# Expert loop of a mixture-of-experts tail: output products by column half, gather split around the second input products

## The chip, the cores and the metric

The program runs on one NeuronCore of a Trainium2 chip, everything in 32-bit floats. The time is the device time of one execution in microseconds (us). The kernel before was run three times: 1990.79, 1992.39 and 1993.29 us. Its trace is of a fourth execution, which took 1992.95 us.

## The reference, cut to what matters

The program is a two-layer mixer block followed by a second block whose feed-forward part is a mixture of 32 experts. Only that part is touched by the change. Each of 256 tokens goes to two experts:

```python
def expert_block(args):
    idx, w, e = args
    xb = tok_pad[idx]                                     # gathered tokens, 1024 wide
    hb = jax.nn.silu(xb @ ex_gate[e]) * (xb @ ex_up[e])   # 1024 -> 512
    return (hb @ ex_down[e]) * w[:, None]                 # 512 -> 1024
...
out = jnp.zeros((n + 1, d), y.dtype).at[tok_buf].add(y.reshape(buf, d))
...
x = _layernorm(ALPHA * x + g2 * ffn, ln2_g[l], ln2_b[l])
```

`g2` is a gate of 1024 values, one for each output column.

## The kernel before, in words

Tokens are sorted into blocks of 64 places (`PLACES`), each with one expert. A first block is done alone; then a loop (`pair_tensor` on TensorE, `pair_scalar` on ScalarE, `pair_vector` on VectorE, `pair_sync` on SyncE) takes two blocks in each iteration. With these inputs it runs 14 iterations. Each engine has its own instruction stream, and semaphores order them. VectorE's loop first counts through the unused steps of 20 possible ones and runs the body in the last 14.

An iteration on TensorE, in program order:

- `in_products(0)`, `in_products(1)` (L3396, L3397): for block j, gate and up products from the gathered tokens `xg`. Each takes a 128x64 tile of the array, one for the lower and one for the upper 64 PSUM partitions, and the two run side by side.
- `gathered(0)` (L3326): half of the gather for the next iteration, as a product of the tokens with the 0/1 matrix `chosen_at`, over the full 128x128 array. VectorE writes `chosen_at` in `choose` (L3507, L3511), in the same iteration.
- `hidden_turned` (L3407) and the transposes of the weights of the places (L3443), full array.
- `out_products(0)`, `out_products(1)` (L3421): for block j, both 512-column halves of the output, again in two 128x64 tiles side by side; block 0 goes to PSUM bank `("down", 0)`, block 1 to `("down", 1)`. In both banks a column half lies on 64 partitions.
- `gathered(1)` (L3326): the second half of the gather.
- four products that put the rows back to their tokens (L3453), full array.

ScalarE does silu (L3481), and copies the transposes and the gather out of PSUM (L3487, L3491). VectorE does gate times up (L3616), four multiplications of 64 partitions by the row of `g2` (L3542), and four additions into the accumulator (L3640).

The weights of an iteration are six transfers of 2048 KB in the order gate and up of block 0, gate and up of block 1, down of block 0, down of block 1, all issued by SyncE at L3306. Each waits until TensorE has used up the same buffer in the iteration before. There is one set of buffers: `("pair_in", 0)` and `("pair_down", 0)` in the tensor `ring`, those of block 1 in `arena`. `pair_groups` gives PSUM banks to the keys in turn, eight banks; `pair_closes` says which group of products frees a weight buffer.

Of the kernel before, what the change touches and what calls it, by code (L numbers as in the profile page):

```python
# [14 lines left out]
ALU = mybir.AluOpType  # L15
# [10 lines left out]
BANK = 512  # L26
# [1488 lines left out]
EC = D_EXPERT // P  # L1515
# [110 lines left out]
PLACES = 64  # L1626
# [20 lines left out]


def pair_groups():
    keys = [("in", 0), ("in", 1), ("xg", 0), ("hidT", 0), ("hidT", 1), ("putT", 0), ("down", 0), ("down", 1), ("xg", 1)]  # L1650
    keys += [("put", tt, hf) for hf in range(2) for tt in range(TT)]
    return keys + [None] * (-len(keys) % BANKS)


def pair_closes():
    return {("in", j): ("pair_in", j) for j in range(2)} | {("down", j): ("pair_down", j) for j in range(2)}


ONE_EVENTS = dict(one_chosen=1, one_weighted=1, one_silu=1, one_hid=1, one_out=2, first_expert=1)
PAIR_EVENTS = dict(weighted=1, silu=2, hid=2, out_low=2, out_high=2)  # L1660


MID_EVENTS = dict(
# [1651 lines left out]
def pair_tensor(pe, K):  # L3315
# [15 lines left out]
    for q in range(2):  # L3331
        pe.wait_ge(K.empty(("xg1", q)), K.empty_count(("xg1", q)))
        for u in range(4):
            kc = 4 * q + u
# [7 lines left out]
    bank = K.bank(("in1", 0))  # L3342
# [42 lines left out]
    with pe.Fori(0, PAIRS) as i, pe.If(i * 2 < blocks):  # L3385
# [21 lines left out]
                ins = pe.transpose(bank[:, n * P:(n + 1) * P], hid[:, q * (EC // 2) + n, :], K.ident)  # L3407
            ins.then_inc(K.full(("hidT", q)), 1)

        def out_products(j):  # L3410

            pe.wait_ge(K.landed(("pair_down", j)), K.landed_count(("pair_down", j), i))
            w = K.pair_w["pair_down", j][0].rearrange("p (k n) -> p k n", k=EC)
            pe.wait_ge(K.empty(("down", j)), K.empty_count(("down", j), i))
            bank = K.bank(("down", j))
            for kc in range(EC):
                if j == 0 and kc % (EC // 2) == 0:
                    q = kc // (EC // 2)
                    pe.wait_ge(K.empty(("hidT", q)), K.drained_count(("hidT", q), i))
                for hf in range(2):  # L3420
                    ins = pe.matmul(bank[hf * PLACES:(hf + 1) * PLACES, :], K.p_hidT[:, kc, j * PLACES:(j + 1) * PLACES],  # L3421
                                    w[:, kc, hf * BANK:(hf + 1) * BANK], start=kc == 0, stop=kc == EC - 1)
            ins.then_inc(K.full(("down", j)), 1)

        def gathered(q):

            pe.wait_ge(K.empty(("xg", q)), K.empty_count(("xg", q), i))
            gather(q, K.bank(("xg", q))).then_inc(K.full(("xg", q)), 1)
# [2 lines left out]

            pe.wait_ge(K.empty(("xg", q)), K.drained_count(("xg", q), i, ago=1))
        in_products(0)
        in_products(1)
        pe.wait_ge(K.sem["chosen_at"], K.count("chosen_at", i, 2))
        gathered(0)
        pe.wait_ge(K.sem["hid"], K.count("hid", i))
        hidden_turned(0)
        hidden_turned(1)
# [4 lines left out]
        ins.then_inc(K.full(("putT", 0)), 1)  # L3444
        out_products(0)
        out_products(1)
        gathered(1)
        pe.wait_ge(K.empty(("putT", 0)), K.drained_count(("putT", 0), i))
        for hf, name in enumerate(("out_low", "out_high")):
            pe.wait_ge(K.sem[name], K.count(name, i))  # L3450
# [112 lines left out]
def pair_vector(dve, K):  # L3563
# [38 lines left out]
    with dve.Fori(0, PAIRS) as step, dve.If(step >= spare):  # L3602
        i = dve.value_load(K.block_expert[0:1, bass.ds(step + (2 * PAIRS + 3), 1)], min_val=0, max_val=PAIRS - 1)
        link = Chain(K.place_done, FIRST_LINKS, i, PLACE_LINKS)
        dve.wait_ge(K.full(("putT", 0)), K.full_count(("putT", 0), i, ago=1))
        dve.wait_ge(K.full(("xg", 1)), K.full_count(("xg", 1), i, ago=1))
        weigh(dve, K, link, 2 * PLACES, "weighted")
        dve.tensor_scalar(K.place, K.place, 2.0 * PLACES, None, ALU.subtract).then_inc(link.sem, 1)
        dve.wait_ge(link.sem, link.count())
        choose(dve, K, link, 0, 2 * PLACES, "chosen_at")  # L3610

        def hidden(j):

            dve.wait_ge(K.sem["silu"], K.count("silu", i, j + 1))
            mine = slice(j * PLACES, (j + 1) * PLACES)
            dve.tensor_tensor(K.p_hid[mine, :], K.p_silu[mine, :], K.bank(("in", j))[mine, :], ALU.mult).then_inc(  # L3616
                K.sem["hid"], 1)
            dve.wait_ge(K.sem["hid"], K.count("hid", i, j + 1))
            dve.sem_inc(K.empty(("in", j)), 1)

        def out(j):

            dve.wait_ge(K.full(("down", j)), K.full_count(("down", j), i))
            for hf, name in enumerate(("out_low", "out_high")):
                gated_output(dve, K, j, hf, K.bank(("down", j))).then_inc(K.sem[name], 1)
            for name in ("out_low", "out_high"):
                dve.wait_ge(K.sem[name], K.count(name, i, j + 1))
            dve.sem_inc(K.empty(("down", j)), 1)

        hidden(0)  # L3630
        hidden(1)
        out(0)
        out(1)

        for hf in range(2):
            for tt in range(TT):
                key = ("put", tt, hf)
                part = K.acc[:, tt, hf * BANK:(hf + 1) * BANK]
                dve.wait_ge(K.full(key), K.full_count(key, i))
                dve.tensor_tensor(part, part, K.bank(key), ALU.add).then_inc(K.empty(key), 1)  # L3640
                dve.wait_ge(K.empty(key), K.drained_count(key, i))
        dve.sem_inc(link.sem, 1)
        link.count()
# [413 lines left out]
```

## Time and profile before

| | |
|---|---|
| median of three runs | 1992.39 us |
| profiled execution | 1992.95 us |
| its span, first to last instruction | 1990.9 us |
| outside the span | 2.05 us |
| expert loop on TensorE | from 1569.66 to 1979.5 us of the span |
| TensorE busy over the span | 1954.6 us (98%) |
| VectorE, ScalarE, GpSimd busy | 1126.6, 468.6, 247.3 us |

TensorE's busy share says little by itself, because the modelled ends of its matmuls overlap. In the loop one has to compare the starts of instructions: how far one iteration's first product lies from the next one's.

### The profile page before, as it was taken

What the parts mean: (1) busy time and instruction counts of PE and PEld (TensorE: products, weight loads), DVE (VectorE), ACT (ScalarE), POOL (GpSimd) and SP (SyncE); (2) the same over time, 40 slices, a digit from 0 to 9 for tenths busy, and PEclk for the clock granted to TensorE, in tenths of its full rate; (3) what the DMA queues carried; (4) which work ended last, traced back from release to release, by engine and by line L of the source; (5) the groups of instructions that cost most, each with busy time, mean ns of one, the idle gap of its engine ahead of it and who ended that gap; (6) DMA issues with size and microseconds to landing.
All of it is one profiled execution on the core that took longest, in us unless ns stands there. A gap on an engine that the chain in (4) does not pass through costs nothing.

```text
span 1990.9 us, 35838 instructions
## 1 busy us (share of the span) xinstructions
PE 1954.6 (98%) x14899; PEld 1353.7 (68%) x14899; DVE 1126.6 (57%) x1898; ACT 468.6 (24%) x904; POOL 247.3 (12%) x238
## 2 busy tenths in 40 slices
PE   8999999999999999999999999999999999999997
PEld 6778979964878978994445555899985444444443
DVE  2697486653569557665568847545447433233324
ACT  3264110001436201000231144433333111110111
POOL 4684000000568100000000001000000000000000
PEclk9999999999999999999999999999998999999999
DMA  8333545454533355536722234200012999999995
GB/s 259 127 127 106 212 151 168 148 196 129 188 127 127 107 212 169 170 128 229 280 85 85 85 127 170 86 4 3 3 48 90 379 428 428 429 428 428 429 428 221
DMA packets 138889, 385.55 MB, mean 194 GB/s; under 512 B 16985, under 2 KB 64449, under 8 KB 127621
## 3 DMA queue, kind: packets, MB, share of 16 engines
q1 hardware_dynamic: 138757, 383.61, 51.4%
q8 instruction: 104, 1.70, 0.4%
q14 instruction: 28, 0.23, 0.0%
HBM read 382.55 MB, written 1.05 MB: 193 GB/s over the span
## 4 chain that ended last, share of the span: by engine, by line
PE 90%; DVE 8%; ACT 1%; issue 1%; DMA 0%; POOL 0%; DVEq 0%; ACTq 0%; POOLq 0%
PE psum L713 13%; PE psum L416 11%; PE psum L1750 10%; PE psum L3396 10%; PE psum L2548 8%; PE psum L3421 5%; PE psum L755 5%; PE psum L3326 3%; PE psum L438 3%; PE psum L609 3%; PE psum L3453 2%; PE psum L674 2%; PE psum L771 2%; PE psum L689 1%; PE psum L2972 1%; PE psum L2617 1%
## 5 line engine op out<-in xcount | busy, mean ns | idle before, releaser
L416 PE MATMUL psum<-arena,ring 128*128 128x256 f32 x1472 | 326.1, 380 | 0.0
L416 PEld LDWEIGHTS psum<-arena,ring 128*128 128x128 f32 x1472 | 276.0, 189 | 46.1 <-issue 7.2
L2548 PE MATMUL psum<-arena 64*64 64x64 f32 (+1 forms) x4320 | 179.8, 238 | 4.5 <-DVE arena L2773 1.8
L2548 PEld LDWEIGHTS psum<-arena 64*64 64x64 f32 x4320 | 171.4, 134 | 6.8 <-issue 2.7
L713 PE MATMUL psum<-arena,ring 128*128 128x128 f32 x1280 | 149.5, 275 | 0.0
L713 PEld LDWEIGHTS psum<-arena,ring 128*128 128x128 f32 x1280 | 146.1, 192 | 0.0
L1750 PE MATMUL psum<-arena,ring 128*128 128x512 f32 (+2 forms) x432 | 142.0, 490 | 0.0
L822 ACT ACTIVATE arena<-psum 128x512 f32<-128x512 f32 (+2 forms) x80 | 42.0, 544 | 347.5 <-PE psum L416 118.8
L1750 PEld LDWEIGHTS psum<-arena,ring 128*128 128x128 f32 (+1 forms) x432 | 81.1, 188 | 60.7 <-issue 55.4
L713 PE MATMUL psum<-arena 128*128 128x128 f32 x960 | 113.7, 274 | 0.0
L713 PEld LDWEIGHTS psum<-arena 128*128 128x128 f32 x960 | 110.4, 192 | 0.0
L2717 ACT ACTIVATE arena<-psum 128x256 f32<-128x256 f32 (+1 forms) x156 | 67.8, 444 | 140.7 <-PE psum L2548 53.1
L3542 DVE TENSOR_TENSOR arena<-psum,arena 64x512 f32<-64x512 f32 x58 | 40.0, 689 | 107.1 <-PE psum L3421 98.9
L3396 PE MATMUL psum<-arena 128*64 128x512 f32 x224 | 99.0, 593 | 0.5
L3396 PE MATMUL psum<-ring,arena 128*64 128x512 f32 x224 | 99.1, 595 | 0.0
L3397 PE MATMUL psum<-ring,arena 128*64 128x512 f32 x224 | 99.1, 595 | 0.0
L3397 PE MATMUL psum<-arena 128*64 128x512 f32 x224 | 99.1, 594 | 0.0
L2347 DVE SCALAR_TENSOR_TENSOR arena<-psum,arena 128x189 f32<-128x189 f32 (+3 forms) x184 | 80.5, 438 | 21.4 <-ACT arena L2083 13.0
L3616 DVE TENSOR_TENSOR arena<-arena,psum 64x512 f32<-64x512 f32 x28 | 19.2, 685 | 121.8 <-ACT arena L3481 121.8
L3396 PEld LDWEIGHTS psum<-arena 128*64 128x64 f32 x224 | 29.7, 136 | 67.0 <-issue 67.0
L3396 PEld LDWEIGHTS psum<-ring,arena 128*64 128x64 f32 x224 | 29.5, 137 | 66.6 <-issue 66.6
L3326 PEld LDWEIGHTS psum<-arena 128*128 128x128 f32 x480 | 55.8, 191 | 23.5 <-issue 23.5
(506 smaller groups left out, 3098.9 us busy)
## 6 DMA issues: line engine op xcount, KB each, us to landing
ring<-in_w_in_dram SPq DMA_DIRECT2D x29, 2048.0 KB, 8.1
ring<-in_ffn_w_dram SPq DMA_DIRECT2D x46, 1024.0 KB, 7.7
arena<-in_ex_gate_dram SPq DMA_DIRECT2D x15, 2048.0 KB, 17.0
arena<-in_ex_up_dram SPq DMA_DIRECT2D x15, 2048.0 KB, 21.3
arena<-in_ex_down_dram SPq DMA_DIRECT2D x15, 2048.0 KB, 22.0
ring<-in_ex_gate_dram SPq DMA_DIRECT2D x14, 2048.0 KB, 14.4
ring<-in_ex_up_dram SPq DMA_DIRECT2D x14, 2048.0 KB, 18.8
ring<-in_ex_down_dram SPq DMA_DIRECT2D x14, 2048.0 KB, 20.5
```

Of the source, the lines that this page charges most:

```text
L416: ins = pe.matmul(bank[:, j, :], w[:, kc, c * P:(c + 1) * P], moving[:, kc, :], start=kc == 0, stop=kc == k - 1)
L438: ins = pe.matmul(bank, K.xT[:, kc, tt * P:(tt + 1) * P], w[:, kc, :], start=kc == 0, stop=kc == DC - 1)
L713: ins = pe.matmul(bank[:, x, w, :], weights(w)[:, k, :], moving[:, k, :], start=k == 0, stop=k == 3)
L755: ins = pe.matmul(K.bank(key), tokens[:, k, :], weights[:, k, :], start=u == k == 0, stop=key[0] == "p" and u == BY_SEVEN - 1 and k == 1)
L1750: ins = pe.matmul(out, a, b, start=i == 0, stop=i == len(pairs_) - 1)
L2347: last = stt(out=o, in0=i, scalar=w, in1=o, op0=ALU.mult, op1=ALU.add)
L2548: ins = pe.matmul(bank[r, u, :], a[r, u], b[r, u], start=i == 0, stop=i == len(terms) - 1)
L2717: act.activation(dst, src, ACT.Copy).then_inc(K.empty(key), 1)
L3326: ins = pe.matmul(bank[:, u * P:(u + 1) * P], K.x_hat[:, tt, kc * P:(kc + 1) * P], K.chosen_at[:, tt, :], start=tt == 0, stop=tt == TT - 1)
L3396: pe.matmul(bank[0:PLACES, :], K.xg[:, kc, mine], low[:, kc, :], start=kc == 0, stop=kc == DC - 1)
L3397: ins = pe.matmul(bank[PLACES:P, :], K.xg[:, kc, mine], high[:, kc, :], start=kc == 0, stop=kc == DC - 1)
L3421: ins = pe.matmul(bank[hf * PLACES:(hf + 1) * PLACES, :], K.p_hidT[:, kc, j * PLACES:(j + 1) * PLACES], w[:, kc, hf * BANK:(hf + 1) * BANK ...
```

## The change

The diff does four things. The second half of the gather moves from behind the output products to in front of the hidden transposes, and the first half moves in front of `in_products(1)`, so that each half stands behind one set of input products. The output products are made by column half: `("down", 0)` gets columns 0 to 511 of both blocks on 128 partitions, `("down", 1)` the rest; both down weights are waited for before the first of them, and both are freed in the last ones. VectorE multiplies by the gate once for each half, 128 partitions at a time. The PSUM banks are handed out in the new order.

```diff
 def pair_groups():
-    keys = [("in", 0), ("in", 1), ("xg", 0), ("hidT", 0), ("hidT", 1), ("putT", 0), ("down", 0), ("down", 1), ("xg", 1)]
+    keys = [("in", 0), ("xg", 0), ("in", 1), ("xg", 1), ("hidT", 0), ("hidT", 1), ("putT", 0), ("down", 0), ("down", 1)]
...
-    return {("in", j): ("pair_in", j) for j in range(2)} | {("down", j): ("pair_down", j) for j in range(2)}
+    return {("in", j): ("pair_in", j) for j in range(2)} | {("down", 1): ("pair_down", 1)}
...
-        def out_products(j):
-
-            pe.wait_ge(K.landed(("pair_down", j)), K.landed_count(("pair_down", j), i))
-            w = K.pair_w["pair_down", j][0].rearrange("p (k n) -> p k n", k=EC)
-            pe.wait_ge(K.empty(("down", j)), K.empty_count(("down", j), i))
-            bank = K.bank(("down", j))
+        def out_products(hf):
+
+            w = [K.pair_w["pair_down", j][0].rearrange("p (k n) -> p k n", k=EC) for j in range(2)]
+            if hf == 0:
+                for j in range(2):
+                    pe.wait_ge(K.landed(("pair_down", j)), K.landed_count(("pair_down", j), i))
+            pe.wait_ge(K.empty(("down", hf)), K.empty_count(("down", hf), i))
+            bank = K.bank(("down", hf))
             for kc in range(EC):
-                if j == 0 and kc % (EC // 2) == 0:
+                if hf == 0 and kc % (EC // 2) == 0:
                     q = kc // (EC // 2)
                     pe.wait_ge(K.empty(("hidT", q)), K.drained_count(("hidT", q), i))
-                for hf in range(2):
-                    ins = pe.matmul(bank[hf * PLACES:(hf + 1) * PLACES, :], K.p_hidT[:, kc, j * PLACES:(j + 1) * PLACES],
-                                    w[:, kc, hf * BANK:(hf + 1) * BANK], start=kc == 0, stop=kc == EC - 1)
-            ins.then_inc(K.full(("down", j)), 1)
+                for j in range(2):
+                    ins = pe.matmul(bank[j * PLACES:(j + 1) * PLACES, :], K.p_hidT[:, kc, j * PLACES:(j + 1) * PLACES],
+                                    w[j][:, kc, hf * BANK:(hf + 1) * BANK], start=kc == 0, stop=kc == EC - 1)
+                    if hf == 1 and kc == EC - 1 and j == 0:
+                        ins.then_inc(K.used_up(("pair_down", 0)), 1)
+            ins.then_inc(K.full(("down", hf)), 1)
...
         in_products(0)
-        in_products(1)
         pe.wait_ge(K.sem["chosen_at"], K.count("chosen_at", i, 2))
         gathered(0)
+        in_products(1)
+        gathered(1)
         pe.wait_ge(K.sem["hid"], K.count("hid", i))
         hidden_turned(0)
         hidden_turned(1)
...
         out_products(0)
         out_products(1)
-        gathered(1)
...
-        def out(j):
-
-            dve.wait_ge(K.full(("down", j)), K.full_count(("down", j), i))
-            for hf, name in enumerate(("out_low", "out_high")):
-                gated_output(dve, K, j, hf, K.bank(("down", j))).then_inc(K.sem[name], 1)
-            for name in ("out_low", "out_high"):
-                dve.wait_ge(K.sem[name], K.count(name, i, j + 1))
-            dve.sem_inc(K.empty(("down", j)), 1)
+        def out(hf, name):
+
+            dve.wait_ge(K.full(("down", hf)), K.full_count(("down", hf), i))
+            dve.tensor_tensor(K.p_out[:, hf, :], K.bank(("down", hf)), K.g_rows[:, 1, hf * BANK:(hf + 1) * BANK], ALU.mult).then_inc(
+                K.sem[name], 1)
+            dve.wait_ge(K.sem[name], K.count(name, i))
+            dve.sem_inc(K.empty(("down", hf)), 1)
```

On TensorE, at the border between the two sets of input products, this stood in a row before (`ring` holds block 0's weights, `arena` block 1's):

```order
L3396 MATMUL psum<-ring,arena 64x512
L3397 MATMUL psum<-ring,arena 64x512
L3390 REGISTER_ALU
L3392 REGISTER_ALU
L3396 MATMUL psum<-arena 64x512
L3397 MATMUL psum<-arena 64x512
```

And this stands there now:

```order
L3396 MATMUL psum<-ring,arena 64x512
L3397 MATMUL psum<-ring,arena 64x512
L3438 REGISTER_ALU
L3431 REGISTER_ALU
L3326 MATMUL psum<-arena 128x128 x8
L3390 REGISTER_ALU
L3392 REGISTER_ALU
L3396 MATMUL psum<-arena 64x512
L3397 MATMUL psum<-arena 64x512
```

The gather (L3326, full array) now stands between two sets of products in 128x64 tiles, and the wait for `chosen_at` (L3438) comes before it.

On TensorE, from the second output products to the end of the iteration, before:

```order
L3412 REGISTER_ALU
L3414 REGISTER_ALU
L3421 MATMUL psum<-arena 64x512 x8
L3427 REGISTER_ALU
L3326 MATMUL psum<-arena 128x128 x8
L3448 REGISTER_ALU
L3453 MATMUL psum<-arena 128x512 x4
L3385 UNCONDITIONAL_BRANCH
```

And now:

```order
L3423 MATMUL psum<-ring,arena 64x512
L3423 MATMUL psum<-arena 64x512
L3423 MATMUL psum<-ring,arena 64x512
L3423 MATMUL psum<-arena 64x512
L3457 MATMUL psum<-arena 128x512 x4
L3385 UNCONDITIONAL_BRANCH
```

The gather is gone from here; the four full-array products L3457 (L3453 before) follow the output products directly.

## Rows read from the trace of the kernel before

**Rows 1.** The page's chain that ended last, and two-megabyte issues of an earlier part

```profile
PE 90%; DVE 8%; ACT 1%; issue 1%; DMA 0%; POOL 0%; DVEq 0%; ACTq 0%; POOLq 0%
...
ring<-in_w_in_dram SPq DMA_DIRECT2D x29, 2048.0 KB, 8.1
```

**Rows 2.** Stretches: us; PE, PEld, DVE, ACT, POOL busy; granted clock; DMA share; GB/s

```profile
1555.00:1600.00 45.00, 43.65 (x218) 20.17 (x216) 14.39 (x28) 5.54 (x12) 0.00 (x0) 1.00 1.01 428
1600.00:1700.00 100.00, 99.97 (x487) 41.46 (x484) 32.48 (x75) 10.21 (x22) 0.00 (x0) 1.00 1.01 428
```

**Rows 3.** The chain in order of time: start us, us, what; starts of iterations

```profile
1569.66 0.57 PE psum L3396
...
1715.16 0.57 PE psum L3396
...
1950.11 0.57 PE psum L3396
...
1957.20 0.64 PE psum L3396
...
1979.54 0.70 DVE arena L3640
```

**Rows 4.** Timeline of SyncE: issues of block 1's up and down weights, last iteration

```profile
1935.72 0.33 SPq L3306 DMA_DIRECT2D arena<-in_ex_up_dram  x1
...
1944.86 0.33 SPq L3306 DMA_DIRECT2D arena<-in_ex_down_dram  x1
```

**Rows 5.** Issue to landing: block 1's gate and up; block 1's down, last iteration

```profile
DMA to landing us min/median/max: 17.0/19.2/21.4
...
DMA to landing us min/median/max: 22.0/22.0/22.0
```

**Rows 6.** Timeline of TensorE, first iteration and start of the second

```profile
1576.08 0.59 PE L3396 MATMUL psum<-ring,arena 128*64 128x512 f32 x1
...
1576.50 0.59 PE L3396 MATMUL psum<-arena 128*64 128x512 f32 x1
...
1582.96 0.59 PE L3396 MATMUL psum<-arena 128*64 128x512 f32 x1
...
1583.49 2.05 PE L3326 MATMUL psum<-arena 128*128 128x128 f32 x16
1585.38 0.65 PE L3407 MATMUL psum<-arena 128*128 128x128 f32 x4
...
1595.16 3.60 PE L3453 MATMUL psum<-arena 128*128 128x512 f32 x8
1598.69 0.64 PE L3396 MATMUL psum<-ring,arena 128*64 128x512 f32 x1
...
1599.17 0.59 PE L3396 MATMUL psum<-ring,arena 128*64 128x512 f32 x1
```

**Rows 7.** Timeline of TensorE, both gather halves of the first block

```profile
1556.31 3.84 PE L3326 MATMUL psum<-arena 128*128 128x128 f32 x32
1559.99 0.38 PE L3356 MATMUL psum<-arena 128*64 128x128 f32 x2
```

**Rows 8.** Timeline of VectorE: first iteration, and the same step in the second

```profile
1575.82 1.11 DVE L3521 TENSOR_SCALAR arena<-arena 128x128 f32<-128x128 f32 x4 [5.37 <-issue]
...
1578.10 0.61 DVE L3511 SCALAR_TENSOR_TENSOR arena<-arena 128x128 f32<-128x128 f32 x2
...
1603.24 0.61 DVE L3511 SCALAR_TENSOR_TENSOR arena<-arena 128x128 f32<-128x128 f32 x2
```

**Rows 9.** Timeline of TensorE: two idle times elsewhere in the program

```profile
1247.10 1.05 PE L1777 MATMUL psum<-arena 128*128 128x2 f32 x8 [2.29 <-ACT arena L2046]
...
1545.59 3.76 PE L3336 MATMUL psum<-arena 128*128 128x64 f32 x32 [1.66 <-DVE arena L3511]
```

**Rows 10.** Stretches after each of these idle times, columns as in rows 2

```profile
1248.40:1251.90 3.50, 3.50 (x19) 1.01 (x11) 3.33 (x6) 0.45 (x1) 0.00 (x0) 0.51 1.05 403
...
1545.60:1549.00 3.40, 3.40 (x31) 3.40 (x31) 3.26 (x7) 0.38 (x1) 0.00 (x0) 1.00 0.54 229
```

More of the change, by code:

```diff
@@ L1655, in pair_closes @@
 def pair_closes():
-    return {("in", j): ("pair_in", j) for j in range(2)} | {("down", j): ("pair_down", j) for j in range(2)}
+    return {("in", j): ("pair_in", j) for j in range(2)} | {("down", 1): ("pair_down", 1)}
 ONE_EVENTS = dict(one_chosen=1, one_weighted=1, one_silu=1, one_hid=1, one_out=2, first_expert=1)
-PAIR_EVENTS = dict(weighted=1, silu=2, hid=2, out_low=2, out_high=2)
+PAIR_EVENTS = dict(weighted=1, silu=2, hid=2, out_low=1, out_high=1)
 MID_EVENTS = dict(
@@ L3619, in hidden @@
             dve.sem_inc(K.empty(("in", j)), 1)
-        def out(j):
-            dve.wait_ge(K.full(("down", j)), K.full_count(("down", j), i))
-            for hf, name in enumerate(("out_low", "out_high")):
-                gated_output(dve, K, j, hf, K.bank(("down", j))).then_inc(K.sem[name], 1)
-            for name in ("out_low", "out_high"):
-                dve.wait_ge(K.sem[name], K.count(name, i, j + 1))
-            dve.sem_inc(K.empty(("down", j)), 1)
+        def out(hf, name):
[4 more added lines that the diff above has]
+            dve.sem_inc(K.empty(("down", hf)), 1)
         hidden(0)
         hidden(1)
-        out(0)
-        out(1)
+        out(0, "out_low")
+        out(1, "out_high")
         for hf in range(2):
```

## The prediction

> **What bounds the kernel now.** I read the page's chain first: TensorE holds 90% of it [rows 1]. The change touches only the expert loop, so I went to the loop's stretches next. They show two resources at their limit at once. TensorE is busy throughout at the full clock (granted 1.00, the 2.4 GHz level), and the 16 DMA engines are at a share of 1.01 and move 428 GB/s without a break [rows 2]. The chain in order of time tells which one sets the pace [rows 3]. From the first product of the loop at 1569.66 to that of the sixth iteration at 1715.16 there are 5 iterations in 145.50 us: **29.10 us** each. From there to the end of the last one (the last addition starts at 1979.54, where a next iteration would have begun within 0.1 us) there are 9 in 264.38 us: **29.38 us** each. The second figure is the stream's: six transfers of 2048 KB are 12.58 MB, and 12.58 MB at 428 GB/s take 29.4 us. So TensorE needs 29.10 us for its work, lives on weights loaded ahead for five iterations, and then waits 0.28 us in each. It waits in front of `in_products(1)`: in the last iteration block 1's up weights are issued at 1935.72 and land 21.4 us later, at 1957.1, and the products start at 1957.20 [rows 3, 4, 5].
>
> The weights come in one unbroken stream, so their landing times stay where they are as long as every transfer is issued early enough. What the change can do is to shift how much of TensorE's own work stands behind a landing, and how long that work is.
>
> **The change, part by part.**
>
> *Products, loads and bytes.* The number and shapes of matmuls per iteration are the same: 32 input, 16 output, 32 gather, 8 put-back records and the transposes. Their own time is a zero in the sum.
>
> *The order around block 1's weights.* Half of the gather (2.0 us with its steps, worked out below) moves in front of the place where TensorE waits. If weights were still the limit, the last iteration would have less work behind each landing. Block 1's up weights are then not the last to be waited for: block 1's down weights land at 1944.86 + 22.0 = 1966.9 [rows 4, 5], and behind them come 16 pairs of output products and 8 put-back records at 0.43 us each and some 0.2 us between them (below), 10.5 us. That gives 1977.4, against 1979.5 now: **-2.1 us**, the most that this edit can bring.
>
> *A wait for `chosen_at` in the first iteration.* VectorE starts the first iteration's steps late, after 5.37 us in which it counts through unused steps, and has `chosen_at` at 1578.10 + 0.61 = 1578.71 [rows 8]. Before, TensorE asked for it behind both input products, at 1583.49. Now it asks behind the first: the last pair of `in_products(0)` starts at 1576.08 [rows 6], and a gather can start 0.53 us later (1582.96 to 1583.49), at 1576.61. With 0.1 to 0.3 us for the signal (0.1 is the landing above to its product) it starts at 1578.9: **+2.3 us**, paid once. Queued behind the waiting gather are `in_products(1)` and all the rest of TensorE's stream, and SyncE's next issues wait for those; nothing else can run ahead. In the second iteration `chosen_at` is there at 1603.24 + 0.61 = 1603.85, and `in_products(0)` begins at 1598.69 and has 16 pairs at 0.43, 6.9 us, so the gather wants it at 1605.7 [rows 6, 8]. Cover: 1.8 us, in this and all later iterations; without it every microsecond of lateness would count 14 times.
>
> *Two more changes of the array's tiling in each iteration.* This is the main term. Input and output products use 128x64 tiles, all else the full array. Pairs of products in 128x64 tiles start 0.42 to 0.43 us apart (1576.08, 1576.50), and two sets of them follow each other without a gap. Where the gather follows a 128x64 pair the distance is 0.53 us, so 0.10 more. The 16 records of a gather then take 1.89 us to the next instruction (1583.49 to 1585.38) [rows 6]. Two gathers in a row take 3.68 (1556.31 to 1559.99) [rows 7], so 16 records with no change of tiling before them take 3.68 - 1.89 = 1.79: again 0.10 less. A step from 128x64 to full thus costs **0.20 us**. The step back: eight put-back records at 0.43 are 3.44, and the next input product comes 3.53 after the first of them; then the second pair comes after 0.48 instead of 0.43 (1598.69, 1599.17) [rows 6]. Together **0.14 us**.
>
> Before, an iteration has four such steps: to the first gather, back to the output products, to the second gather, back to the next iteration. Now it has six, since the first gather stands between two sets of 128x64 products (+0.20 + 0.14). The step behind the output products stays but leads to put-back products of 512 columns; its second half lies between the 0.05 of a 512-column record and the 0.10 of a gather's, so I take 0.02 off. Net **+0.32 us** per iteration, bounds 0 and 0.40.
>
> The Trainium skill, on the page "TensorEngine Tiling (Array Packing)", section "Key Properties", says that changing the tiling mode, not merely the tile, drains the array. The trace agrees with it at each of these borders and adds the price. The page gives none; if one took the roughly 128 cycles of pipe drain that "TensorE: Matmul & The Clock Gate" names under "Phases on the wall clock" as an estimate, 28 extra steps would be 1.5 us in place of the 4.5 us of the rows.
>
> *What becomes of the waits for weights.* TensorE's work is then 29.42 us, which is above the stream's 29.38. So it no longer waits for weights at all: the 9 x 0.28 = **-2.5 us** are saved. Both down weights are now needed at once, some 19 us after the iteration's start (32 pairs at 0.43, two gathers of 1.99, a step back, and under a microsecond of transposes); in the last one that is 1569.7 + 2.3 + 13 x 29.42 + 19 = 1973, long after 1966.9.
>
> *Later frees.* Down weights of block 1 are freed about 2.3 us later in the iteration than now (a gather half and two steps stand ahead of them), those of block 0 another 3.4 us later (8 pairs more), 5.7 in all. Issue to landing is now 22.0 us [rows 5] where a transfer on an idle stream needs 8.1 [rows 1], so 13.9 us of queue stand ahead; 5.7 of them go, the stream stays unbroken, cost 0.
>
> *VectorE.* Four multiplications of 64 partitions become two of 128. The row of a 128-partition addition reads 0.70 us [rows 3], so nothing grows, and 1.4 us leave VectorE where it is not awaited. Before, a gather half covered the last multiplications. Now the low half is done under the high half's products, and the high one (0.1 + 0.7 + 0.1 us) under the low put-back products (half of 3.44, so 1.7). Cost 0; without that cover 0.9 us each iteration.
>
> **Sum.** 2.3 + 14 x 0.32 - 2.5 = **+4.3 us**. The same from the other side: 1569.66 + 2.3 + 14 x 29.42 = 1983.8 against 1979.5. The trace's own execution took 1992.95 (span 1990.9 and 2.05 around it), so it would be 1997.3; the median shown lies 0.56 lower, hence 1996.7. What a measurement of this kernel can tell from no change is about 0.2%, or 4.0 us.
>
> **Rivals.**
>
> *A, as above.* +4.3, own range 1995.7 to 1997.7 by 0.05 us either way on the step. Chance 0.46.
>
> *B, the clock falls.* The first iteration's wait is an idle TensorE of about 2.3 us. Elsewhere in this trace 2.29 us of idleness are followed by a granted clock of 0.51 over 3.5 us (the 1.2 GHz level), while 1.66 us are followed by 1.00 [rows 9, 10]. Before the first, though, TensorE's work was thinner than here. Half speed over such a stretch does 1.7 us less work: +6.0, 1998.4. Chance 0.24.
>
> *C, the tiling steps cost nothing more.* They might be hidden by the queue when the neighbours change. Then TensorE needs 29.10 again, the 2.3 us are paid, and it ends at 1569.66 + 2.3 + 407.4 = 1979.4: -0.1, 1992.2. Against it speaks that the gap is there at every border of this kind that I looked at. Chance 0.12. With half the price TensorE still stays under the stream's pace, but the lead of weights lasts: +2, 1994.4, chance 0.07.
>
> *D, the other sign.* The gather hides in the wait for weights, and the wait for `chosen_at` is absorbed. The place is the front of `in_products(1)`, the price is the -2.1 above, and it decides if the steps cost under 0.02 us and VectorE's first steps come 2 us earlier than in the trace. Nothing on VectorE's path changes ahead of them. 1990.3, chance 0.02; even then it is within 0.2%.
>
> *E, `chosen_at` is late in every iteration*, because VectorE's end of an iteration moves: 1.8 us of cover gone and 0.5 more would be +7 on top. Its additions stay tied to the same put-back products. Chance 0.08, 2000 and above.
>
> **Numbers.** Slower by over 0.2%: two thirds of A (its range is cut by the line at +4.0), all of B and E: 0.63. Within 0.2%: the rest of A, C and D: 0.36. Faster: 0.01, kept for what none of these cases holds. The range leaves out E and the lower half of C's first case: 1992.6 to 1999.2.
>
> **What the next profile would show.** Iterations of 29.42 us from first to last, with no change of pace at the sixth; 29.10 would prove C. In the first iteration the gather L3326 at 1578.9 with some 2.2 us of idle time behind VectorE's L3515. A gather followed by the first product of block 1 after 1.89 us, and that product's successor after 0.48. The last landing still at about 1966.9, with the put-back products now ending 17 us after it. The forecast is wrong if a step is priced otherwise between new neighbours, or if a stretch at half clock follows the wait.

## The result and the profile after

The changed kernel takes **2001.41 us** (median of 10 runs, 1997.88 to 2004.71), the kernel before 1992.53 us (10 runs, 1990.79 to 1998.55). The ratio is 1.0042, with a 95% interval of 1.0031 to 1.0053: slower by 8.4 us, 6.2 to 10.6 (the two medians lie 8.9 us apart). The forecast was 1996.7 us, 4.3 us slower, with a range up to 1999.2, so the sign was right and the size was half of what came.

The profiled execution of the changed kernel took 2004.71 us, its span is 2002.7 us. Its chain in order of time shows the last products ahead of the loop, the starts of the second, third and last iteration and, in the last row, the loop's end; they answer to [rows 3]:

```profile
1570.31 3.68 PE psum L3380 x8
...
1607.32 0.57 PE psum L3396
...
1636.86 0.57 PE psum L3396
...
1961.72 0.57 PE psum L3396
...
1991.29 0.70 DVE arena L3643
```

From the second iteration to the last there are 12 in 354.40 us, **29.53 us** each, and there is no change of pace at the sixth. The stream's pace of 29.38 us [rows 3] is gone: TensorE waits for no weights. The products ahead of the loop end at 1570.31 + 3.68 = 1573.99, so the first iteration took **33.3 us**. The page's chain still has TensorE at the head, answering to [rows 1]:

```profile
PE 89%; DVE 7%; issue 1%; ACT 1%; DVEq 0%; DMA 0%; POOL 0%; ACTq 0%
```

The timeline of TensorE shows the first iteration's border, then the same places of the second (rows for the upper half of the products, which start 0.01 to 0.04 us later, left out); compare [rows 6]:

```profile
1580.40 0.59 PE L3396 MATMUL psum<-ring,arena 128*64 128x512 f32 x1
...
1583.15 3.41 PE L3326 MATMUL psum<-arena 128*128 128x128 f32 x16 [2.16 <-DVE arena L3515]
1586.50 0.87 PE L3396 MATMUL psum<-arena 128*64 128x512 f32 x1
...
1587.20 0.59 PE L3396 MATMUL psum<-arena 128*64 128x512 f32 x1
...
1613.74 0.59 PE L3396 MATMUL psum<-ring,arena 128*64 128x512 f32 x1
...
1614.27 2.05 PE L3326 MATMUL psum<-arena 128*128 128x128 f32 x16
1616.25 0.64 PE L3396 MATMUL psum<-arena 128*64 128x512 f32 x1
...
1616.73 0.59 PE L3396 MATMUL psum<-arena 128*64 128x512 f32 x1
```

The gather of the first iteration waits 2.16 us for VectorE's L3515, as forecast. But it then takes 3.35 us to the next product, where the second iteration's takes 1.98. The stretches (us; PE, PEld, DVE, ACT, POOL busy; granted clock; DMA share; GB/s) tell why:

```profile
1578.00:1581.00 3.00, 3.00 (x14) 0.72 (x10) 0.87 (x4) 0.00 (x0) 0.00 (x0) 1.00 1.01 431
1581.00:1583.20 2.20, 0.04 (x1) 0.05 (x1) 2.10 (x9) 0.59 (x1) 0.00 (x0) 1.00 0.95 357
1583.50:1587.00 3.50, 3.50 (x18) 3.07 (x18) 0.11 (x1) 0.00 (x0) 0.00 (x0) 0.51 1.02 393
...
1600.00:1700.00 100.00, 99.68 (x472) 42.64 (x470) 30.83 (x71) 9.29 (x21) 0.00 (x0) 1.00 1.00 420
```

Behind the idle time TensorE is granted 0.51 of its clock, the 1.2 GHz level, for about 3.4 us. That costs 1.6 us: the first iteration is 3.8 us longer than the others, and 2.2 of it is the wait. In the last row the stream moves 420 GB/s where [rows 2] have 428: it has become the follower.

Steps of the tiling in the second iteration: 0.53 us from the last 128x64 pair to the gather, 1.98 through the gather, 0.48 to the second pair behind it. With 0.43 for a pair and 1.79 for a gather without steps that is 0.10 + 0.19 + 0.05 = 0.34, the 0.20 + 0.14 of the forecast.

### The profile page after: what moved, and what is told of

It is laid out like the page before. It is cut to its first block, busy times and chain, and to the rows that moved or that the text cites. A ratio compares the mean times of both kernels' runs of the same rounds, so it can differ in the third digit from the quotient of the medians.

```text
span 2002.7 us, 35824 instructions
## 1 busy us (share of the span) xinstructions
PE 1964.0 (98%) x14899; PEld 1365.0 (68%) x14899; DVE 1108.0 (55%) x1870; ACT 466.8 (23%) x904; POOL 245.7 (12%) x238
## 4 chain that ended last, share of the span: by engine, by line
PE 89%; DVE 7%; issue 1%; ACT 1%; DVEq 0%; DMA 0%; POOL 0%; ACTq 0%
PE psum L713 12%; PE psum L416 11%; PE psum L1750 10%; PE psum L3396 9%; PE psum L2548 8%; PE psum L3423 5%; PE psum L755 5%; PE psum L3326 3%; PE psum L438 3%; PE psum L3457 3%; PE psum L609 3%; PE psum L674 2%; PE psum L771 2%; PE psum L689 1%; PE psum L2972 1%
## 5 line engine op out<-in xcount | busy, mean ns | idle before, releaser
L713 PEld LDWEIGHTS psum<-arena 128*128 128x128 f32 x960 | 110.4, 192 | 0.0
L3423 PE MATMUL psum<-ring,arena 128*64 128x512 f32 x224 | 98.7, 593 | 1.5
L3396 PE MATMUL psum<-arena 128*64 128x512 f32 x224 | 99.6, 596 | 0.0
L3397 PE MATMUL psum<-arena 128*64 128x512 f32 x224 | 99.6, 596 | 0.0
L3423 PE MATMUL psum<-arena 128*64 128x512 f32 x224 | 99.1, 595 | 0.0
L3397 PE MATMUL psum<-ring,arena 128*64 128x512 f32 x224 | 99.1, 595 | 0.0
L3396 PE MATMUL psum<-ring,arena 128*64 128x512 f32 x224 | 99.1, 595 | 0.0
L3485 ACT ACTIVATE arena<-psum 64x512 f32<-64x512 f32 x28 | 16.5, 591 | 349.2 <-PE psum L3397 349.2
L3628 DVE TENSOR_TENSOR arena<-psum,arena 128x512 f32<-128x512 f32 x28 | 19.3, 691 | 110.1 <-PE psum L3423 110.1
## 6 DMA issues: line engine op xcount, KB each, us to landing
ring<-in_ex_up_dram SPq DMA_DIRECT2D x14, 2048.0 KB, 13.5
```

The source lines that it names most:

```text
L713: ins = pe.matmul(bank[:, x, w, :], weights(w)[:, k, :], moving[:, k, :], start=k == 0, stop=k == 3)
L3396: pe.matmul(bank[0:PLACES, :], K.xg[:, kc, mine], low[:, kc, :], start=kc == 0, stop=kc == DC - 1)
L3397: ins = pe.matmul(bank[PLACES:P, :], K.xg[:, kc, mine], high[:, kc, :], start=kc == 0, stop=kc == DC - 1)
L3423: ins = pe.matmul(bank[j * PLACES:(j + 1) * PLACES, :], K.p_hidT[:, kc, j * PLACES:(j + 1) * PLACES], w[j][:, kc, hf * BANK:(hf + 1) * BAN ...
```

## The experiments

Each profile gives the pace of its loop to 0.01 us; a median also holds what the clock did ahead of the loop, and the loop's start differs from one profile to the next by up to 4 us, by 7 in e7's (below). So pace and loop are the sharper measure, and the median is beside it. The ratio is to the kernel before, run again in the same round (its medians there are 1992.66 to 1993.22 us). Line numbers shift by a few with an edit. Diffs are against the changed kernel, unless another is named.

| kernel | median us (runs) | ratio [95%] | first iteration, then pace | loop's start to end |
|---|---|---|---|---|
| before | 1992.53 (10) | | 29.10 x5, then 29.38 | 1569.6 to 1979.5 |
| changed | 2001.41 (10) | 1.0042 [1.0031, 1.0053] | 33.3, then 29.53 | 1573.9 to 1991.3 |
| e1 output by block | 2011.65 (4) | 1.0092 [1.0072, 1.0112] | 32.6, then 30.40 | 1572.1 to 2000.0 |
| e2 output by half alone | 1993.26 (10) | 0.9996 [0.9987, 1.0006] | 29.10 | 1573.6 to 1981.0 |
| e3 both gathers behind | 1993.95 (10) | 1.0006 [0.9994, 1.0018] | 31.5, then 29.10 | 1573.1 to 1982.9 |
| e4 `chosen_at` early | 1997.79 (10) | 1.0022 [1.0007, 1.0036] | 30.0, then 29.53 | 1570.1 to 1984.1 |
| e5 two more steps | 2007.01 (4) | 1.0066 [1.0042, 1.0089] | 33.8, then 29.88 | 1573.2 to 1995.5 |
| e6 down waits early | 2000.41 (5) | 1.0037 [1.0023, 1.0050] | 31.9, then 29.53 | 1573.2 to 1989.1 |
| e7 first gather in front | 1992.85 (11) | 1.0002 [0.9991, 1.0013] | 29.6, then 29.10 (between input products) | 1576.7 (gather) to 1986.6 |
| e8 e4 and e6 | 2002.71 (4) | 1.0047 [1.0029, 1.0066] | 30.0, then 29.53 | 1573.4 to 1987.5 |
| e9 one wait at the product | 1996.71 (10) | 1.0018 [1.0009, 1.0028] | 29.9, then 29.45 | 1570.8 to 1983.5 |
| e10 before, started later | 1993.24 (11) | 1.0004 [0.9995, 1.0014] | 29.10 | 1572.1 to 1979.6 |
| e11 changed, started later | 2000.75 (5) | 1.0042 [1.0029, 1.0056] | 31.8, then 29.53 | 1571.5 to 1987.3 |

### e1: the gather's halves as changed, the output by block as before

```diff
-                    ins = pe.matmul(bank[j * PLACES:(j + 1) * PLACES, :], K.p_hidT[:, kc, j * PLACES:(j + 1) * PLACES],
+                    ins = pe.matmul(bank[hf * PLACES:(hf + 1) * PLACES, :], K.p_hidT[:, kc, j * PLACES:(j + 1) * PLACES],
...
-        out(0, "out_low")
-        out(1, "out_high")
+        out(0)
+        out(1)
```

The whole of `out_products`, `out` and the frees are those of before.

> The gather stays split around block 1's input products as in the changed kernel; output products and gate multiplications go back to one block at a time. Theory S (steps of the array's tiling): the pace is set by the two extra steps, so an iteration takes 29.10 + 0.34 = 29.44 us, against 29.53 in the changed kernel (the 0.10 that its output products wait longer at their start goes away), and the first iteration's wait for chosen_at of 2.2 us stays. Some 1.4 us less than the changed kernel, 6 more than before. Theory W (the output products by half are the cause): the pace falls back to 29.10, then 29.38, and the kernel is within 2.5 us of before.

The pace is 30.40 us, 0.87 over the changed kernel's, where one theory had it 0.09 under and the other at 29.10: both missed a cost. The timeline of VectorE and that of TensorE show the end of an iteration:

```profile
1630.72 1.41 DVE L3542 TENSOR_TENSOR arena<-psum,arena 64x512 f32<-64x512 f32 x2 [2.03 <-PE psum L3421]
1632.64 0.69 DVE L3640 TENSOR_TENSOR arena<-arena,psum 128x512 f32<-128x512 f32 x1 [0.51 <-PE psum L3453]
...
1631.50 3.67 PE L3453 MATMUL psum<-arena 128*128 128x512 f32 x8 [0.82 <-issue]
```

TensorE sits idle for 0.82 us before the put-back products, since their right-hand side is the output that VectorE is still multiplying by the gate (1.41 us for the last block's two halves). Before, the second half of the gather filled that time. In the changed kernel each half is one multiplication:

```profile
1633.27 0.69 DVE L3628 TENSOR_TENSOR arena<-psum,arena 128x512 f32<-128x512 f32 x1 [2.75 <-PE psum L3423]
...
1633.16 3.70 PE L3457 MATMUL psum<-arena 128*128 128x512 f32 x8
```

The put-back of the low half starts at 1633.16, before the high half's multiplication (1633.27). So the output by column half is what pays for moving the gather away; the two edits belong together.

### e2: only the output by column half; the gather where it was

```diff
-    keys = [("in", 0), ("xg", 0), ("in", 1), ("xg", 1), ("hidT", 0), ...
+    keys = [("in", 0), ("in", 1), ("xg", 0), ("hidT", 0), ("hidT", 1), ("putT", 0), ("down", 0), ("down", 1), ("xg", 1)]
...
+        in_products(1)
         pe.wait_ge(K.sem["chosen_at"], K.count("chosen_at", i, 2))
         gathered(0)
-        in_products(1)
-        gathered(1)
...
         out_products(1)
+        gathered(1)
```

> The kernel before with only its output products and gate multiplications by column half; the gather stays where it was, its second half behind the output products. Theory S: four tiling steps and a late question for chosen_at as before, so TensorE's own work is 29.10 us, at most 29.2, and the loop ends where the stream of weights lets it: same time as before within 1 us. Theory W (waiting for both down weights at once costs): 0.1 us or more in each iteration over the stream's 29.38, 1.5 us or more in all.

Same time as before, and 29.10 us from first to last:

```profile
1573.64 0.57 PE psum L3396
1602.74 0.57 PE psum L3396
...
1951.94 0.57 PE psum L3396
1981.08 0.70 DVE arena L3643
```

Four steps of the tiling in an iteration, TensorE's pace of before. The output by half costs nothing by itself, though both theories had expected 29.38 from the stream. Its loop starts 4.0 us later than before's profile and ends only 1.5 us later; e10 takes that up.

### e3: both gather halves behind `in_products(1)`

```diff
         in_products(0)
+        in_products(1)
         pe.wait_ge(K.sem["chosen_at"], K.count("chosen_at", i, 2))
         gathered(0)
-        in_products(1)
         gathered(1)
```

> As the changed kernel, but both gather halves stand behind block 1's input products: four tiling steps in an iteration, as before the change, and chosen_at is asked for late. Theory S: TensorE's own work is 29.10 + 0.10 (the later start of the output products) = 29.2 us, under the stream's 29.38, so the loop is as long as before: 29.38 in the late iterations, no idle time for chosen_at, same time as before within 1 us. Theory W: 29.5 us in each iteration as in the changed kernel, and 5 us or more over before.

Same as before within 0.06% (interval -0.06% to 0.18%), pace 29.10 us: with four steps of the tiling again (and, by its order of banks, a single wait at the first output product; see e9) all of the 0.43 us is gone. The 31.5 us of its first iteration come from the clock, in the stretch from before the loop into it:

```profile
1570.80:1577.60 6.80, 6.80 (x16) 1.90 (x16) 1.85 (x3) 0.00 (x0) 0.00 (x0) 0.52 1.01 431
```

### e4: `chosen_at` built before the weights of the places

```diff
+        choose(dve, K, link, 2 * PLACES, 2 * PLACES, "chosen_at")
...
-        choose(dve, K, link, 0, 2 * PLACES, "chosen_at")
```

> As the changed kernel, but VectorE makes chosen_at ahead of the place weights (it compares with slots 128 higher and subtracts afterwards), 1.7 us earlier. Theory S with the clock as a second part: the idle time in front of the first gather falls from 2.2 to about 0.4 us, the clock doesn't fall behind it, and the loop is 1.8 us shorter, or 3.5 where the changed kernel's clock fell; the pace stays at 29.53. If the clock had fallen for another reason, only 1.8 us go and the first iteration still holds a stretch at half clock.

The first gather now waits 0.41 us in place of 2.16, no stretch at the lower clock follows it in this profile (granted 1.00 from 1577.5 to 1595), and the rest of the loop runs at the same 29.53:

```profile
1577.58 2.05 PE L3326 MATMUL psum<-arena 128*128 128x128 f32 x16 [0.41 <-DVE arena L3515]
1579.56 0.64 PE L3396 MATMUL psum<-arena 128*64 128x512 f32 x1
```

The first iteration falls from 33.3 to 30.0 us: 1.75 us of it is the wait, 1.6 the clock. The medians differ by 3.6, in two rounds of runs.

### e5: two more steps of the tiling in each iteration

```diff
+                if j == 1 and kc == DC // 2:
+                    gather(0, K.bank(("xg", 0)), (2, 3)).then_inc(K.full(("xg", 0)), 1)
...
-        gathered(0)
+        pe.wait_ge(K.empty(("xg", 0)), K.empty_count(("xg", 0), i))
+        gather(0, K.bank(("xg", 0)), (0, 1))
```

> As the changed kernel, but the first gather half is cut in two, and its second part stands in the middle of block 1's input products: two more tiling steps in each iteration, no other work. Theory S: 29.53 + 0.34 = 29.87 us an iteration, 4.8 us more than the changed kernel. If a step's price belongs to the waits and register instructions at the borders and not to the tiling, there is none of them at the new borders: no change, 29.53.

The first half of the gather is cut in two, with half of block 1's input products between. The chain's starts of the second and third iteration:

```profile
1607.08 0.57 PE psum L3398
...
1636.96 0.57 PE psum L3398
```

29.88 us against 29.53: **0.35 us** for one step to the full array and one back, where 0.34 was the forecast's price. The number of products is the same, and no wait or register instruction stands at the new borders.

### e6: the waits for both down weights ahead of the hidden transposes

```diff
-            if hf == 0:
-                for j in range(2):
-                    pe.wait_ge(K.landed(("pair_down", j)), K.landed_count(("pair_down", j), i))
...
         gathered(1)
+        for j in range(2):
+            pe.wait_ge(K.landed(("pair_down", j)), K.landed_count(("pair_down", j), i))
         pe.wait_ge(K.sem["hid"], K.count("hid", i))
```

> As the changed kernel, but TensorE waits for both down weights ahead of its wait for the hidden layer, so that one wait and its register instructions less stand between the transposes and the output products. If the 0.10 us by which the output products start later than before (0.38 against 0.28 us behind the last transpose) is work of TensorE's sequencer between these two points, the pace is 29.44 us instead of 29.53, 1.3 us less in all. If it is ScalarE's copy of the first transpose that they wait for, nothing changes: 29.53.

The pace stays at 29.53 us. That the waits for weights stand in front of the output products is not what is missing from the sum. e8, which is e4 with this edit, has the pace of e4.

### e7: the first half of the gather at the head of the iteration

```diff
-        in_products(0)
         pe.wait_ge(K.sem["chosen_at"], K.count("chosen_at", i, 2))
         gathered(0)
+        in_products(0)
         in_products(1)
         gathered(1)
```

(and VectorE builds `chosen_at` for the next iteration at its end.)

> A version that keeps the output products by half and has the tiling steps of the kernel before: the first gather half stands ahead of block 0's input products, right behind the put-back products of the iteration before (full array next to full array, no step), the second behind block 1's. VectorE makes chosen_at one iteration ahead, for the first iteration before the loop; the down weights are waited for early. Theory S: four steps, 29.10 us of work, no idle time for chosen_at, and 2 us less work behind the last landing of block 1's up weights: the loop ends at the landing of the last down weights plus 10.5 us, 1977.4 for a loop that starts at 1569.6, 2.1 us less than before (0.1%). If work behind the last landings does not set the end, the same time as before.

There the first half follows the full-array put-back products, so the iteration is back at four steps, and at 29.10 us. The time is that of before, 0.02% more with an interval of -0.09% to 0.13%: a gather half now stands ahead of the loop's first input product, and in its profile the clock was at 0.50 as the loop began. That profile is the slowest of the 11 executions, with a loop that began 7.1 us later than before's, so it cannot show the 2.1 us that the expectation had for an early start. The median does not show them either.

### e8 and e9: e4 and e6 together, then with a single wait at the first output product

```diff
+        pe.wait_ge(K.empty(("down", 0)), K.empty_count(("down", 0), i))
         pe.wait_ge(K.sem["hid"], K.count("hid", i))
...
-            pe.wait_ge(K.empty(("down", hf)), K.empty_count(("down", hf), i))
+            if hf == 1:
+                pe.wait_ge(K.empty(("down", hf)), K.empty_count(("down", hf), i))
```

(This diff is e9's against e8.)

> The edits of the two runs before it together: chosen_at made ahead of the place weights, and the down weights waited for early. Theory S: what is left of the loss are the two extra tiling steps alone, 29.44 us an iteration against the stream's 29.38, and 0.5 us in the first: the loop ends some 3 us later than before (1982.5 against 1979.5 if it starts at the same time). Were there another cost that I have not named, it would be over 4.

> The kernel with the early chosen_at and the early down-weight waits, with one more edit: TensorE's wait for bank ("down", 0) also stands ahead of the hidden transposes, so that the first output product carries a single wait (that for the second copy of hidT). Theory: in the changed kernel the product carried two waits, so one of them became an instruction of its own in the sequencer, and the products started 0.09 us later (0.145 behind the end of the copy in place of 0.055). Then the pace falls from 29.53 to 29.44 us, and the time is 1.3 us less than with the early waits alone. Rival: the later start comes from something else, such as which instruction the copy's semaphore is attached to; the pace stays 29.53.

e8 is at 29.53 us, where 29.44 was expected, so a cost was still unnamed; e9 is at **29.45**. How the instruction stands in TensorE's stream, first in the changed kernel, then in e9:

```
L3423 MATMUL psum<-ring,arena 64x512 [waits bank4_drained,bank7_drained]
...
L3421 MATMUL psum<-ring,arena 64x512 [waits bank4_drained]
```

And the timelines, the changed kernel's first:

```profile
1625.61 0.66 ACT L3491 ACTIVATE arena<-psum 128x256 f32<-128x256 f32 x2 [1.61 <-PE psum L3407]
1625.65 0.38 PE L3448 MATMUL psum<-arena 128*128 128x128 f32 x2
1626.11 0.13 PEld L3423 LDWEIGHTS psum<-ring,arena 128*64 128x64 f32 x1 [0.31 <-issue]
1626.14 0.61 PE L3423 MATMUL psum<-ring,arena 128*64 128x512 f32 x1
```

e9's:

```profile
1618.96 0.66 ACT L3492 ACTIVATE arena<-psum 128x256 f32<-128x256 f32 x2 [1.62 <-PE psum L3407]
1619.00 0.38 PE L3449 MATMUL psum<-arena 128*128 128x128 f32 x2
1619.40 0.13 PEld L3421 LDWEIGHTS psum<-ring,arena 128*64 128x64 f32 x1 [0.25 <-ACT arena L3492]
1619.40 0.64 PE L3421 MATMUL psum<-ring,arena 128*64 128x512 f32 x1
```

From the start of the transposes of the places' weights to the first output product it is 0.49 us in the changed kernel and 0.40 in e9, with the same products and the same copy by ScalarE between. The product waits for that copy in both; with two semaphores to wait for it starts 0.09 us later. In the compiled program of the changed kernel the wait for the copy (`bank4_drained`) is an instruction of its own in front of the product, which itself waits for `bank7_drained`; in e9 the product itself waits for the copy, as in the kernel before, e2, e3 and e7. The edit changes both at once, the number of waits and where the late one stands, so it does not tell which of the two has the price. The loop's length agrees: 414.0 us in e8, 412.7 in e9. The medians lie 6 us apart, but only 1.2 of them are this edit; e9's loop also started 2.7 us earlier in its profile.

### e10 and e11: the loop started later, before and changed

```diff
+        if q == 1:
+            gather(q, K.bank(("first", q)))
```

The edit stands in the first block, whose second gather half is then computed twice.

> The kernel before, with the second gather half of the first block computed twice ahead of the loop: 16 more matmul records, about 1.8 us of TensorE time; the output is unchanged. Theory (the stream absorbs lateness): the weights' landings set the last nine iterations, so that a start of the loop 1.8 us later only uses up the 2.5 us of waits. In a profile whose loop would start at 1569.6 it starts at 1571.4 and the loop's end stays within 0.5 us of 1979.5; if the loop starts late anyway (1573), 29.10 us throughout and the whole 1.8 us is paid. Time between +0 and +1.8 us, nearer to +1.8 if late starts are the usual case. Rival: nothing is absorbed, +1.8 us always, and iterations of 29.38 stay.

> The changed kernel, with the second gather half of the first block computed twice ahead of the loop, about 1.8 us of TensorE time more; the output is unchanged. Theory: its loop is bound by TensorE alone, 29.53 us an iteration against 29.38 of the stream, so nothing is absorbed: the loop's end moves by 1.8 us and the time is 1.8 us over the changed kernel's 2001.4, 2003.2. The first wait for chosen_at would be shorter by the 1.8 us if VectorE started as before, but VectorE's count of unused steps starts from the first block's products as well, so the wait stays at some 2 us. Rival: the wait for chosen_at shrinks by the delay, and the time stays at 2001.4 or falls, since the clock would not fall behind a short wait.

e10 answers for the kernel before. Its chain:

```profile
1572.20 0.57 PE psum L3398
...
1601.30 0.57 PE psum L3398
...
1950.50 0.57 PE psum L3398
...
1979.64 0.70 DVE arena L3642
```

It starts 2.5 us later than before's [rows 3] and ends 0.10 us later. All 13 iterations to the last start take 29.10 us; none waits for weights. Of the 2.54 us that TensorE lost ahead of the loop 2.44 came back, because before they were spent as waits, 0.28 us in each of nine iterations.

In e11 the loop starts at 1571.5 and ends at 1987.3; 29.53 behind the first iteration. That is 415.7 us, the changed kernel's 417.3 without the 1.6 of its lower clock, so nothing comes back in its iterations. Its median does not tell +1.8 from 0, since the interval of the ratio is 2.7 us either way. And here the first wait, equally long, is not followed by the lower clock. Nor is it in e1 (last two rows):

```profile
1580.76 2.05 PE L3326 MATMUL psum<-arena 128*128 128x128 f32 x16 [2.16 <-DVE arena L3517]
...
1578.50:1580.70 2.20, 0.10 (x2) 0.00 (x0) 2.10 (x10) 0.59 (x1) 0.00 (x0) 1.00 1.01 432
1580.80:1587.00 6.20, 6.20 (x36) 3.30 (x38) 0.42 (x1) 0.00 (x0) 0.00 (x0) 1.00 1.00 425
...
1581.32 2.05 PE L3326 MATMUL psum<-arena 128*128 128x128 f32 x16 [2.16 <-DVE arena L3511]
...
1581.30:1587.00 5.70, 5.68 (x34) 3.21 (x36) 0.48 (x1) 0.00 (x0) 0.00 (x0) 1.00 1.00 382
```

In e5 it is, as in the changed kernel:

```profile
1582.46 1.15 PE L3326 MATMUL psum<-arena 128*128 128x128 f32 x8 [2.16 <-DVE arena L3518]
...
1583.00:1587.00 4.00, 4.00 (x16) 1.45 (x16) 0.00 (x0) 0.00 (x0) 0.00 (x0) 0.59 1.04 442
```

So the same 2.16 us of idleness were followed by half the clock in two profiles (changed, e5) and by the full one in two others (e1, e11).

## Why the prediction was wrong in size

**The bound, right.** Before, TensorE's work is 29.10 us and the stream sets 29.38. e2, e3, e7 and e10 show 29.10 wherever the weights are far enough ahead.

**The steps of the tiling, right.** 0.20 + 0.14 us forecast; 0.34 read in the changed kernel, 0.35 from e5. Rivals C, its half-price form and D fall. One sign was named wrongly: the gather takes 1.98 us to the next product and not 1.89, since the first part of the step back stands there, as it did in the forecast's own "two gathers of 1.99". The 0.02 taken off at the put-back products should not have been: from the last output pair (1632.63) they start 0.53 later, where a pair takes 0.43, and the eight of them take 3.63 us to the next input product where 3.53 stood before; together 0.20 again. The timeline of the changed kernel (the start of the put-back products, 1633.16, stands at e1):

```profile
1632.63 0.59 PE L3423 MATMUL psum<-arena 128*64 128x512 f32 x1
...
1636.79 0.64 PE L3396 MATMUL psum<-ring,arena 128*64 128x512 f32 x1
```

**"Net +0.32 us per iteration", the term that failed: too low by 0.11.** The pace is 29.53, not 29.42. 0.02 is the item above, 0.09 is the second wait at the first output product, which the forecast did not have: the bank handed out to `("down", 0)` is waited for at the product beside ScalarE's copy, where before another instruction in front of it took that wait. e9 shows it, and e3, whose product has one wait, is back at 29.10. Times 14 the 0.11 is 1.5 us.

**The wait for `chosen_at`, right.** 2.16 us measured, 2.3 forecast. Cover in later iterations held, so rival E falls: the gather of the second starts 0.53 us behind the products.

**Rival B, the clock, came true in the profile, on top of A: the second step that failed.** The main sum put 2.3 us of idleness into the loop and nothing for the clock behind it; 1.6 us were measured there, 1.7 was the rival's price, and its chance 0.24. It came in two of the four profiles with this wait (not in e1 and e11); what decides it, no run here shows.

**"The 9 x 0.28 = -2.5 us are saved", true only where the loop starts early.** The changed kernel waits for no weights, and against before's profile, whose loop began at 1569.66, the saving is there (2.4 us in the account below). But the forecast took this one start for all. Ahead of the loop the clock falls at other places from one execution to the next. The changed kernel's profile has it at 0.55 in this stretch, before's (second row) at 1.00:

```profile
1545.00:1556.00 11.00, 11.00 (x44) 7.38 (x46) 7.71 (x29) 2.05 (x3) 0.00 (x0) 0.55 0.75 287
...
1545.00:1556.00 11.00, 10.41 (x64) 5.85 (x64) 8.32 (x31) 2.05 (x3) 0.00 (x0) 1.00 0.55 205
```

Before's had fallen earlier, to 0.57 over 1531 to 1539. The changed kernel's loop begins 4.3 us later than before's; in e2, e3, e6 and e8 it begins 3.5 to 4.0 later too. With a late start the order of before runs at 29.10 us throughout and absorbs up to 2.4 us of the lateness (e10, the kernel before: 2.4 of 2.5; e2, with its steps of the tiling: 2.4 of 4.0). The changed kernel, at 29.53 against the stream's 29.38, absorbs nothing. So the waits of before are also a slack that hides late starts, and the changed kernel has given it up.

**The account.** For the two profiled loops: 2.2 + 14 x 0.43 - 2.4 + 1.6 (clock) = 7.4 us, and 417.3 against 409.9 is 7.4. The forecast had 4.3 for the same items; the 3.1 between them are 1.5 of pace and 1.6 of clock. Either of them alone would have left the forecast inside its range (1998.2 or 1998.3 us), both together give 1999.8. The executions differ by 11.8 us since the changed kernel's also started its loop 4.3 late. For a late start the -2.4 goes: 2.2 + 6.0 = 8.2 without and 9.8 with the lower clock in the loop; for an early one 5.8 and 7.4. The measured 8.4 (6.2 to 10.6) lies among them.

How often each case comes is not shown, since only one execution of each kernel has a trace, but in e4 at least late starts are not the rule. In all thirteen profiles the loop ends 13.4 us (13.5 in one) before the execution's time. Eight of e4's ten executions took 1995.71 to 1997.99 us, so their loops ended at 1982.3 to 1984.6; at e4's 414.0 us of loop they began at 1568.3 to 1570.6, about where before's did, if none of them had the lower clock inside the loop. Each execution also has its mean granted clock beside its time. At 0.993 or more, the changed kernel's executions (6 of 10) have a median of 1999.8 us and those of before (36 in the rounds of e1 to e11) 1992.3: 7.5 us with much of the clock's part taken out. How the median's 8.4 divides between late starts, the clock behind the wait and noise stays open.

**"The last landing still at about 1966.9", wrong without cost.** SyncE issues the last down weights at 1958.73, and the DMA view gives 13.8 us to their landing:

```profile
1958.73 0.33 SPq L3306 DMA_DIRECT2D arena<-in_ex_down_dram  x1
...
arena<-in_ex_down_dram SPq DMA_DIRECT2D x1, 2048.0 KB, 13.8
```

That is 1972.5, 5.6 us later than forecast: the stream now goes at TensorE's pace. The products that need them start 19 us into the last iteration, at about 1980.5, so 8 us of cover are left. "Later frees, cost 0" held.

**VectorE, right, but the price of the missing cover was seen only from one side.** "Cost 0; without that cover 0.9 us each iteration": e1 is that case, with 0.87.

No version here beats the kernel before. e7, e3 and e2 equal it, all with four steps of the tiling.

## What to carry to other kernels

When a loop waits a little for a stream in each iteration, those waits are a reserve that can absorb lateness from ahead of it; a change that fills them with work loses the reserve, so compare it with a late start as well as with the profiled one. Count changes of the array's tiling in an iteration as instructions with a price, and place full-array work beside other full-array work. When work is moved from in front of a product, look which waits that product then carries, and what the moved work had covered behind it (e1: a gate multiplication of VectorE, 0.87 us each iteration).

## What the runs showed of the hardware

- A pair of steps between 128x64 tiles and the full array costs 0.34 to 0.35 us in 32-bit floats, whether 8 or 16 records stand between them (e5, the changed kernel). The Trainium skill, "TensorEngine Tiling (Array Packing)", section "Key Properties", says that a change of the tiling mode drains the array. That each change costs time agrees with it; the runs add the price.
- A matmul that has two semaphores to wait for, the late one in an instruction of its own, started 0.09 us later than one that waits for the late one alone (0.49 against 0.40 us from the same point, e9 against the changed kernel).
- Behind 2.16 us of idleness the clock fell in two profiles (0.51 over 3.5 us in the changed kernel's, 0.59 over 4.0 us in e5's) and stayed at 1.00 in two others (e1, e11).
